# A float32 hybrid decoder trunk on one core: four small moves in order, banks and tables

## The chip, the core and the metric

The kernel runs on one core of a Trainium2 chip. The metric is device time in microseconds (us) of one execution, and the smaller is the better. The engines are named as in the profile: PE (TensorE, matmuls; PEld its weight loads), DVE (VectorE), ACT (ScalarE), POOL (GpSimd), SP (SyncE, which issues the DMAs of the weights).

## The reference

Two layers over 272 tokens (16 learned meta tokens and 256 others) of 1024 numbers, all in float32. Each layer norms its input, multiplies it by `w_in`, and splits the product into query latents (384), key-value latents (256), a rotary key (32), and the two halves of a recurrence (`xr` and `gt`, 512 each):

```python
for l in range(DEPTH):
    u = rmsnorm(h, norm_mix_g[l])
    cq, ckv, kr, xr, gt = jnp.split(u @ w_in[l], SPLITS, axis=-1)
    att = mla_mixer(cq, ckv, kr, cos, sin, ...)   # latents normed, 8 heads, causal blocks (0,16) (16,144) (144,272)
    rnn = rglru_mixer(xr, gt, ...)                # convolution, gates sigmoid(xb @ w_a), scan, times gelu(gt)
    h = h + concat(rmsnorm(att), rmsnorm(rnn)) @ w_out[l]
    u = rmsnorm(h, norm_ffn_g[l])
    h = h + (swiglu(u) if l % 2 == 0 else moe_swiglu(u))   # layer 0 dense, layer 1: top 2 of 8 experts
return h[:, N_META:]
```

The softmax of a head and query block is exp(s - max s) over its keys, divided by the sum. The cosine and sine of the rotary angles are computed once, from `positions`.

## The kernel before

**Matmuls of split floats.** Every large float32 weight is loaded by SP into one of four slots `raw`. ACT copies a piece of it, rounded, into `whi` (`split`, L984), DVE computes the rest `wlo` = `raw` - `whi` (`lo`, L1436), and PE makes three passes: high by high, high by low, low by high (L668 to L670 for the mixers and the dense part, L2551 and L2576 for the experts' first and second product). A piece can be split once the piece four before it in the ring has been used by PE; a slot of `raw` is free once its last `wlo` is done.

**Order.** Each engine has its own program, and the order of its instructions is the order of the code; nothing is scheduled by a tool. Engines wait on semaphores. The 8 PSUM banks are given out by `plan_blocks`: a block without a bank takes the next of banks 0 to 3 in turn, others are given one by hand (`GT_BANK`, `P_BANK`, `OUT_BANK`). PE waits in `fill` until the bank's last reader has signalled `emptied[bank]`.

**The part of a mixer where the latents are normed** (both layers). The blocks of `w_in` are computed in the order q, kv, kr, xr 0 to 3, gt 0. The first norm's root is a Sqrt on ACT (L1011). Behind block xr 1, PE sums the squares of the latents (`latss`). On ACT, each turn of the loop at L1071 splits the pieces that are due (`mix(l, *later(k))`). In the turn of (xr, 1), behind those splits, stand `tables()` (layer 0 alone: Sin of two angles, L1036 and L1038, and an Exp, L1040, that signals `splus_e`) and an empty `mark(ACT.Tanh)` of one element (L958), there for its table. In the turn of (xr, 2), ahead of the splits, stands `root_rows` (L1018), the Sqrt of the latents' sums. DVE takes the reciprocal of that root (`rows`, L1453) behind its own low piece of (xr, 1). PE, behind block xr 3, waits for it, spreads it over the partitions (`cqbc` and `kvbc`, L2047), computes gt 0, and goes on to the queries (L2156), for which DVE has multiplied the latents (L1513). Then come the recurrence's two sets of gates (L2175), four blocks each in the turning banks, which ACT empties with Tanh (L1113). Behind them ACT takes Exp of the decays (L1123), which waits for `vec_done`: 26 small operations on POOL (L843 to L857) that begin when `splus_e` is signalled.

**Attention.** `ATTENTION` lists the order per layer. `score(t)` (L2263) makes one block per head and query tile t, in the turning banks; DVE (`maxima`, L1598) adds the mask, scales and takes the maximum of a head in one custom instruction, ACT takes Exp with its sum per head (L1177). Tile 0 is the 16 meta tokens, and is computed in layer 0 alone. Between them DVE empties the `gt` blocks (`gelu_gate`, L1488) and computes the gate's gelu (L1681 to L1687). `values(t)` turns the probabilities of each head through PE (L2307, blocks `p` in banks 6, 7, 2 in turn), DVE and ACT by turns copy them out (`turned`, L1616 and L1187), and PE multiplies them by the values (L2322). DVE's program is written out by hand there: `gelu_gate(3)`, `gelu_times(1)`, then `turned(1, 0)`.

**Experts.** Each of the 8 experts runs 24 pieces: 16 of gate and up (L2551), then 8 of down (L2576) in `down(16)` to `down(23)`. The activated hidden state is turned through PE in two parts (L2563). ACT copies the second part's high half (`heh`, L1354) behind piece 19, and DVE subtracts it for the low half (`hel`, L1956) behind its own piece 19. Eleven chunks of 128 hidden units stand in the pieces of down; the last expert takes the pieces in another order (`in_turn`), so that its output's first half is done early, and there PE needs the second part of the turned state ahead of `down(18)`:

```python
down(17)
if gathers is not None:
    gather_low(gathers)
if not is_last(e):
    down(18, 19)
pe.wait_ge(xr_free[1], n0[1] + 3)     # hel is there
pe.wait_ge(xr_free[0], n0[0] + 4)
if is_last(e):
    down(18, 19)
down(20, 21, 22, 23)
```

## Time and profile before

| | |
|---|---|
| time, median of 3 runs | 895.87 us (894.41 to 896.41) |
| the profiled execution, its own time | 898.03 us |
| its span in the profile | 896.2 us |
| PE busy | 866.8 us (97%) |
| DVE busy | 683.6 us (76%) |
| ACT busy | 576.0 us (64%) |
| POOL busy | 70.8 us (8%) |
| granted TensorE clock, mean | 0.985 of full speed |
| moved by DMA | 208.70 MB, mean 233 GB/s |

The span goes from the first to the last recorded instruction or transfer; the execution's own time is 1.8 us longer. Matmuls are pipelined in the profile, so that PE's busy time is not a measure of its speed. The mixer of layer 0 lies at 0 to 150 us, the dense part up to 358 us, the mixer of layer 1 up to 486 us, and the experts take the rest.

### The profile page before, as it was taken

Reading aid. Unit: us, or ns where it says so; the run is one execution under the profiler, and the core shown is the slowest. Engines: PE = TensorE matmul, PEld = TensorE weight load, DVE = VectorE, ACT = ScalarE, POOL = GpSimd, SP = SyncE. Lnnn points to the kernel's source line nnn. Section 1 sums busy time; section 2 is a strip of 40 time slices with the busy share of each in tenths; the row PEclk is TensorE's granted clock in tenths of the full one; section 3 lists DMA queues with packets and bytes.
Section 4 is the critical chain, followed back from the end, with each engine's and each line's share of the span. In section 5 each row is a group of like instructions: output and inputs, shape, how many; then the busy total and the mean of one; then the engine's idle time right before and its main releaser. Section 6 shows DMA issues by size and latency. Waiting matters only on the chain.

```text
span 896.2 us, 15435 instructions
## 1 busy us (share of the span) xinstructions
PE 866.8 (97%) x5827; PEld 794.5 (89%) x5827; DVE 683.6 (76%) x914; ACT 576.0 (64%) x782; POOL 70.8 (8%) x93
## 2 busy tenths in 40 slices
PE   8989899999999999999899999999999999999995
PEld 7855789999999999965799989999998989999994
DVE  5667867766666555677877889789897998789883
ACT  6666746555454443666746777787778777777762
POOL 3530010000000000000042000000000000000001
PEclk9999899999999999999999999999999999999998
DMA  9505025555578553405055799899998999899981
GB/s 314 189 2 185 17 95 165 173 179 187 167 199 240 144 170 112 142 19 170 13 206 182 261 362 371 324 348 404 345 405 302 372 391 361 314 353 402 353 346 26
DMA packets 119436, 208.70 MB, mean 233 GB/s; under 512 B 5968, under 2 KB 71760, under 8 KB 119376
## 3 DMA queue, kind: packets, MB, share of 16 engines
q1 hardware_dynamic: 117232, 201.79, 63.7%
q0 software_dynamic: 1568, 5.24, 2.9%
q10 hardware_dynamic: 576, 0.87, 0.4%
q8 instruction: 38, 0.62, 0.3%
q14 instruction: 22, 0.18, 0.1%
HBM read 202.65 MB, written 5.24 MB: 232 GB/s over the span
## 4 chain that ended last, share of the span: by engine, by line
PE 85%; DVE 6%; ACT 4%; DMA 3%; issue 2%; POOL 0%; ACTq 0%; DVEq 0%; POOLq 0%; SPq 0%
PE ps L2551 27%; PE ps L2576 12%; PE ps L668 11%; PE ps L670 11%; PE ps L669 10%; PE ps L2156 2%; PE ps L2516 2%; DVE wlo L1436 2%; PE ps L2263 2%; PE ps L2322 1%; DMA raw<-in_w_in_dram 1%; PE ps L2047 1%; PE ps L2563 1%; DMA raw<-in_moe_w_down_dram 1%; DVE rr L1453 1%
## 5 line engine op out<-in xcount | busy, mean ns | idle before, releaser
L1436 DVE TENSOR_TENSOR wlo<-raw,whi 128x1536 fp32r<-128x1536 f32 (+4 forms) x298 | 437.9, 1495 | 90.5 <-ACT whi L984 88.2
L984 ACT ACTIVATE whi<-raw 128x1536 fp32r<-128x1536 f32 (+4 forms) x298 | 374.7, 1275 | 128.6 <-PE ps L670 58.1
L668 PE MATMUL ps<-uhi,whi 128*128 128x272 f32 (+1 forms) x576 | 170.3, 296 | 0.6 <-DVE wlo L1436 0.6
L670 PE MATMUL ps<-uhi,wlo 128*128 128x272 f32 (+1 forms) x576 | 166.8, 290 | 0.0
L669 PE MATMUL ps<-ulo,whi 128*128 128x272 f32 (+1 forms) x576 | 166.5, 289 | 0.0
L2551 PE MATMUL ps<-whi,xeh 128*128 128x320 f32 (+1 forms) x512 | 125.0, 325 | 0.0
L2551 PE MATMUL ps<-whi,xel 128*128 128x320 f32 (+1 forms) x512 | 123.5, 322 | 0.0
L2551 PE MATMUL ps<-wlo,xeh 128*128 128x320 f32 (+1 forms) x512 | 123.5, 322 | 0.0
L668 PEld LDWEIGHTS ps<-uhi,whi 128*128 128x128 f32 (+1 forms) x576 | 109.0, 189 | 4.2 <-issue 2.2
L669 PEld LDWEIGHTS ps<-ulo,whi 128*128 128x128 f32 (+1 forms) x576 | 109.2, 190 | 0.6
L670 PEld LDWEIGHTS ps<-uhi,wlo 128*128 128x128 f32 (+1 forms) x576 | 108.9, 189 | 0.0
L2551 PEld LDWEIGHTS ps<-whi,xeh 128*128 128x128 f32 x512 | 88.5, 188 | 0.7
L2551 PEld LDWEIGHTS ps<-wlo,xeh 128*128 128x128 f32 x512 | 89.0, 188 | 0.0
L2551 PEld LDWEIGHTS ps<-whi,xel 128*128 128x128 f32 x512 | 89.0, 188 | 0.0
L2576 PE MATMUL ps<-whi,heh 128*128 128x512 f32 x176 | 70.5, 401 | 2.4 <-DVE hel L1956 2.4
L2576 PE MATMUL ps<-wlo,heh 128*128 128x512 f32 x176 | 70.2, 399 | 0.0
L2576 PE MATMUL ps<-whi,hel 128*128 128x512 f32 x176 | 70.1, 399 | 0.0
L668 PE MATMUL ps<-ahi,whi 128*128 128x272 f32 x176 | 50.8, 289 | 0.0
L669 PE MATMUL ps<-alo,whi 128*128 128x272 f32 x176 | 50.7, 288 | 0.0
L670 PE MATMUL ps<-ahi,wlo 128*128 128x272 f32 x176 | 50.6, 287 | 0.0
L2576 PEld LDWEIGHTS ps<-whi,heh 128*128 128x128 f32 x176 | 33.4, 190 | 10.1 <-DVE hel L1956 2.9
L2576 PEld LDWEIGHTS ps<-whi,hel 128*128 128x128 f32 x176 | 33.4, 190 | 8.1
(314 smaller groups left out, 1200.3 us busy)
## 6 DMA issues: line engine op xcount, KB each, us to landing
raw<-in_moe_w_down_dram SPq DMA_DIRECT2D x24, 1536.0 KB, 9.2
raw<-in_moe_w_gate_dram SPq DMA_DIRECT2D x16, 1536.0 KB, 7.5
raw<-in_moe_w_up_dram SPq DMA_DIRECT2D x16, 1536.0 KB, 8.5
raw<-in_moe_w_gate_dram SPq DMA_DIRECT2D x16, 1280.0 KB, 10.1
raw<-in_moe_w_up_dram SPq DMA_DIRECT2D x16, 1280.0 KB, 9.4
raw<-in_ffn_w_gate_dram SPq DMA_DIRECT2D x11, 1024.0 KB, 5.2
raw<-in_ffn_w_up_dram SPq DMA_DIRECT2D x11, 1024.0 KB, 5.2
raw<-in_ffn_w_down_dram SPq DMA_DIRECT2D x8, 1408.0 KB, 6.9
```

The costliest lines, as they stand in the source:

```text
L668: pe.matmul(dst, wh, xh, start=start, stop=False, skip_group_check=True)
L669: pe.matmul(dst, wh, xl, start=False, stop=False, skip_group_check=True)
L670: return pe.matmul(dst, wl, xh, start=False, stop=stop, skip_group_check=True)
L984: act.activation(placed(whi, s, src), src, ACT.Copy).then_inc(hi_done, 1)
L1436: dve.tensor_tensor(placed(wlo, s, src), src, placed(whi, s, src).bitcast(F32), ALU.subtract).then_inc(lo_done, 1)
L1453: dve.reciprocal(rr[0:n, :], rr[0:n, :]).then_inc(rows_done, 1)
L2047: return pe.matmul(ps[0:width, bk, 0:T], ident[:, row:row + 1].to_broadcast([P, width]), rr[:, :], start=True, stop=True)
L2156: q = pe.matmul(bank(b, slice(width * i, width * (i + 1))), wq[:, k, c:c + width], cq[:, k, :], start=(k == 0), stop=(k == QC - 1), skip_g ...
L2263: pe.matmul(ps[0:n, b.bank, 0:lead + n], qT[0:QKH, h, lead:lead + n], kT[0:QKH, h, 0:lead + n], start=True, stop=True).then_inc(filled, 1)
L2516: m = pe.matmul(ps[:, b, c * 2 * P:(c + 1) * 2 * P], part[:, t * D + at:t * D + at + P], onehot[:, t, :, :], start=(t == 0), stop=(t == 1))
L2551: q = pe.matmul(ps[:, 2 * kind + n, 0:width], xs[:, kk, half, :], w[:, sl, at:at + width], start=(kk == 0 and xs is xeh and w is whi), sto ...
L2576: q = pe.matmul(ps[:, 4 + n, :], xs[:, kk, :], w[:, sl, at:at + 512], start=(kk == 0 and xs is heh and w is whi), stop=(kk == FEC - 1 and ...
```

## The change

Four edits:

1. On ACT, `tables()` and `mark(ACT.Tanh)` stand in the turn of (xr, 2), behind its split; so `root_rows` comes ahead of them, in both layers.
2. `GT_BANK` has a row per layer; in layer 1 the block gt 3 goes to bank 5, not 7.
3. The scores of the meta tokens (layer 0) are one block in bank 6: eight matmuls of 16 columns side by side. DVE masks, scales, takes the maxima and subtracts them in four operations over 16 x 8 x 16; ACT takes one Exp over them all, without a sum; DVE sums in `averages(0)`. The mask is added before the scale as before.
4. In the last expert, DVE computes the turned state's low half (`turned(6, TURN_B, 2)`) between pieces 18 and 19.

```diff
--- before.py
+++ after.py
@@ -208,7 +208,7 @@
 AHEAD = 2
 WARM = 5
 P_BANK = (6, 7, 2)
-GT_BANK = (6, 5, 4, 7)
+GT_BANK = ((6, 5, 4, 7), (6, 5, 4, 5))
 N_FF = 2 * (FF // GC) + KD
 MIX0 = [0, PER_MIX + N_FF]
 SPLIT0 = [0, MIX_SPLIT + 2 * N_FF]
@@ -258,10 +258,10 @@
             add("kbc", h)
         for what, t in ATTENTION[l]:
             if what == "scores":
-                for h in range(NH):
-                    add("s", t, h)
+                for h in range(NH if t else 1):
+                    add("s", t, h, bank=None if t else 6)
             elif what == "gt":
-                add("gt", t, bank=GT_BANK[t])
+                add("gt", t, bank=GT_BANK[l][t])
             elif what == "meta":
                 add("p", t, META, bank=6)
             elif what == "values":
@@ -1079,7 +1079,7 @@
                         act.activation(u32[:, QC:QC + KVC, :], ckv[:, :, :], ACT.Square).then_inc(squares, 1)
                         act.activation(kr[NOPE:QKH, 2, :], kr[NOPE:QKH, 0, :], ACT.Square).then_inc(krsq_done, 1)
                     mix(l, *later(k))
-                    if (name, c) == ("xr", 1):
+                    if (name, c) == ("xr", 2):
                         if not l:
                             tables()
                         mark(ACT.Tanh)
@@ -1199,6 +1199,10 @@
 
                 def exponentials(t, after=None):
                     act.wait_ge(sc_done, len(tiles(0)) * l + tiles(l).index(t) + 1)
+                    if not t:
+                        s = scores[0][0:NMETA, :, 0:NMETA]
+                        act.activation(s, s, ACT.Exp).then_inc(exp_done, NH)
+                        return
                     for h in range(NH):
                         exponential(t, h)
                         if after is not None:
@@ -1587,9 +1591,29 @@
 
                 dve.wait_ge(qscale_done, l + 1)
 
+                def meta_maxima():
+
+                    n = NMETA
+                    m0 = C_MASK + T - P
+                    b = B[l, "s", 0, 0]
+                    s = scores[0][0:n, :, 0:n]
+                    mask = con[0:n, m0:m0 + n].rearrange("p (h k) -> p h k", h=1).to_broadcast([n, NH, n])
+
+                    def of_head(row):
+                        return row.rearrange("p (h k) -> p h k", k=1).to_broadcast([n, NH, n])
+
+                    dve.wait_ge(filled, b.ready())
+                    dve.tensor_tensor(s, ps[0:n, b.bank, 0:NH * n].rearrange("p (h k) -> p h k", h=NH), mask, ALU.add)                       .then_inc(emptied[b.bank], 1)
+                    dve.wait_ge(emptied[b.bank], b.before + 1)
+                    link(dve.tensor_tensor(s, s, of_head(rt[0:n, 0, :]), ALU.mult))
+                    link(dve.tensor_reduce(small[0:n, 0, 0, :], s, AX.X, ALU.max))
+                    dve.tensor_tensor(s, s, of_head(small[0:n, 0, 0, :]), ALU.subtract).then_inc(sc_done, 1)
+
                 def maxima(t):
 
                     lead, n = TILES[t]
+                    if not t:
+                        return meta_maxima()
                     keys = lead + n
                     m0 = C_MASK + T - P - lead
                     for h in range(NH):
@@ -1620,6 +1644,8 @@
                     n = TILES[t][1]
                     o = osb_of(t)
                     dve.wait_ge(exp_done, NH * (len(tiles(0)) * l + tiles(l).index(t) + 1))
+                    if not t:
+                        link(dve.tensor_reduce(small[0:n, 0, 2, :], scores[0][0:n, :, 0:n], AX.X, ALU.add))
                     link(dve.reciprocal(small[0:n, t, 3, :], small[0:n, t, 2, :]))
                     b = B[l, "o", t]
                     dve.wait_ge(filled, b.ready())
@@ -1988,8 +2014,13 @@
                     turned(0, TURN_A, 1)
                     w(e, p, 16, 17)
                     times_up(1, HALF_B // 2)
-                    w(e, p, 18, 19)
-                    turned(6, TURN_B, 2)
+                    if is_last(e):
+                        w(e, p, 18)
+                        turned(6, TURN_B, 2)
+                        w(e, p, 19)
+                    else:
+                        w(e, p, 18, 19)
+                        turned(6, TURN_B, 2)
                     w(e, p, 20, 21, 22, 23)
                     if more:
                         w(e + 1, p, 0, 1, 2)
@@ -2252,8 +2283,22 @@
 
                 pe.wait_ge(qrot_done, l + 1)
 
+                def meta_scores():
+
+                    n = NMETA
+                    b = B[l, "s", 0, 0]
+                    fill(pe, b)
+                    for h in range(NH):
+                        kb = B[l, "kbc", h]
+                        pe.wait_ge(emptied[kb.bank], kb.before + 1)
+                        q = pe.matmul(ps[0:n, b.bank, n * h:n * (h + 1)], qT[0:QKH, h, 0:n], kT[0:QKH, h, 0:n],
+                                      start=True, stop=True)
+                    q.then_inc(filled, 1)
+
                 def score(t):
                     lead, n = TILES[t]
+                    if not t:
+                        return meta_scores()
                     for h in range(NH):
                         b = B[l, "s", t, h]
                         fill(pe, b)
```

ACT's program in layer 0, from the squares of the latents to the split ahead of the queries; before:

```order
L1080 ACTIVATE kr<-kr 32x272
L984 ACTIVATE whi<-raw 128x1024 x2
L1036 ACT_TABLE_LOAD
L1036 ACTIVATE sinT<-rope 128x272
L1038 ACTIVATE cosT<-rope 128x272
L1040 ACT_TABLE_LOAD
L1040 ACTIVATE spt<-spt 128x8
L958 ACTIVATE scr<-one 128x1
L1018 ACT_TABLE_LOAD
L1018 ACTIVATE rr<-ps,eps 64x272
L958 ACTIVATE scr<-one 128x1
L984 ACTIVATE whi<-raw 128x1024 x2
```

and with the change:

```order
L1080 ACTIVATE kr<-kr 32x272
L984 ACTIVATE whi<-raw 128x1024 x2
L1018 ACTIVATE rr<-ps,eps 64x272
L958 ACTIVATE scr<-one 128x1
L984 ACTIVATE whi<-raw 128x1024
L1036 ACT_TABLE_LOAD
L1036 ACTIVATE sinT<-rope 128x272
L1038 ACTIVATE cosT<-rope 128x272
L1040 ACT_TABLE_LOAD
L1040 ACTIVATE spt<-spt 128x8
L958 ACTIVATE scr<-one 128x1
L984 ACTIVATE whi<-raw 128x1024
```

The latents' root (L1018) with its mark stands three table loads and four activations sooner and has no load of its own; of the two splits behind it (L984) one has moved ahead of the tables. Further on, the load that stood at the gates' first Tanh (L1113) is gone as well, in both layers; in layer 1 the one at `mark(ACT.Tanh)` now stands behind the root.

DVE's program for the last expert, from the pieces 16 and 17 to its end; before:

```order
L1436 TENSOR_TENSOR wlo<-raw,whi 128x1536 x2
L1970 SCALAR_TENSOR_TENSOR hact<-act,slotg,ps 128x640
L1436 TENSOR_TENSOR wlo<-raw,whi 128x1536
L1436 TENSOR_TENSOR wlo<-raw,whi 128x1024
L1956 TENSOR_TENSOR hel<-ps,heh 128x512
L1956 TENSOR_TENSOR hel<-ps,heh 128x128
L1436 TENSOR_TENSOR wlo<-raw,whi 128x1536 x3
L1436 TENSOR_TENSOR wlo<-raw,whi 128x1024
```

and with the change:

```order
L1440 TENSOR_TENSOR wlo<-raw,whi 128x1536 x2
L1996 SCALAR_TENSOR_TENSOR hact<-act,slotg,ps 128x640
L1440 TENSOR_TENSOR wlo<-raw,whi 128x1536
L1982 TENSOR_TENSOR hel<-ps,heh 128x512
L1982 TENSOR_TENSOR hel<-ps,heh 128x128
L1440 TENSOR_TENSOR wlo<-raw,whi 128x1024
L1440 TENSOR_TENSOR wlo<-raw,whi 128x1536 x3
L1440 TENSOR_TENSOR wlo<-raw,whi 128x1024
```

The two subtractions for `hel` (L1956, in the change L1982) stand ahead of the 128x1024 piece, which is piece 19.

DVE's program at the meta tokens' scores, behind gt 1, its beginning before (the pair of L1598 comes eight times, once per head):

```order
L1488 TENSOR_TENSOR gt<-ps,rsb 128x272
L1529 ISA
L1598 ISA u,small<-ps,con,rt 16x16
L1598 ISA small 16x1
L1598 ISA u,small<-ps,con,rt 16x16
L1598 ISA small 16x1
L1598 ISA u,small<-ps,con,rt 16x16
```

and with the change, down to the next tile's first pair:

```order
L1492 TENSOR_TENSOR gt<-ps,rsb 128x272
L1533 ISA
L1606 TENSOR_TENSOR u<-ps,con 16x8x16
L1608 TENSOR_TENSOR u<-u,rt 16x8x16
L1609 TENSOR_REDUCE small<-u 16x8
L1610 TENSOR_TENSOR u<-u,small 16x8x16
L1622 ISA u,small<-ps,con,rt 128x144
L1622 ISA small 128x1
```

Sixteen custom instructions and the sign's turn (L1606) have become four operations.

## Rows read from the trace of the kernel before

**Rows 1.** The page: the chain that ended last, shares of the span by engine
```profile
PE 85%; DVE 6%; ACT 4%; DMA 3%; issue 2%; POOL 0%; ACTq 0%; DVEq 0%; POOLq 0%; SPq 0%
```

**Rows 2.** Waits of PE over the whole run: us in total, times, longest
```profile
PE ps L2047 <- DVE rr L1453: 3.1, 2, 2.9
...
PE ps L2576 <- DVE hel L1956: 2.4, 1, 2.4
PE ps L2307 <- DVE gt L1488: 2.4, 1, 2.4
PE ps L2175 <- ACT ta L1113: 2.1, 2, 1.1
```

**Rows 3.** Timeline of ACT, layer 0: start, us, engine line op, [idle before <- releaser]
```profile
38.79 1.28 ACT L1036 ACT_TABLE_LOAD   x1
...
43.75 0.48 ACT L1018 ACTIVATE rr<-ps,eps 64x272 f32<-64x272 f32 x1
...
59.16 1.28 ACT L1113 ACT_TABLE_LOAD   x1
...
63.61 2.12 ACT L1123 ACTIVATE xr<-ta,nsp 128x272 f32<-128x272 f32 x4
```

**Rows 4.** Timeline of DVE, layer 0, at the latents' root
```profile
44.50 1.84 DVE L1453 RECIPROCAL rr<-rr 64x272 f32<-64x272 f32 x1 [1.79 <-ACT scr L958]
```

**Rows 5.** Timeline of PE, layer 0: block xr 2's first matmul, and the spread
```profile
37.26 0.39 PE L668 MATMUL ps<-uhi,whi 128*128 128x272 f32 x1
...
46.40 2.18 PE L2047 MATMUL ps<-rr,con 128*128 128x272 f32 x4 [2.87 <-DVE rr L1453]
```

**Rows 6.** Stretches: length, busy of PE, PEld, DVE, ACT, POOL, clock, DMA share, GB/s
```profile
60.00:63.00 3.00, 2.01 (x8) 1.43 (x8) 0.00 (x0) 2.99 (x8) 0.00 (x0) 1.00 0.00 0
382.60:386.87 4.27, 4.18 (x32) 3.87 (x36) 4.20 (x10) 1.02 (x1) 0.08 (x1) 1.00 0.01 4
46.40:52.10 5.70, 5.70 (x32) 5.09 (x36) 5.60 (x11) 0.00 (x0) 4.66 (x13) 0.72 0.00 0
```

**Rows 7.** Timeline of DVE, layer 1, at the latents' root
```profile
380.80 1.84 DVE L1453 RECIPROCAL rr<-rr 64x272 f32<-64x272 f32 x1
```

**Rows 8.** Timeline of POOL: the chain behind `splus_e`, its first, an inner one, its last
```profile
42.45 0.37 POOL L843 TENSOR_SCALAR spt<-spt 128x8 f32<-128x8 f32 x1 [8.70 <-ACT spt L1040]
...
46.71 1.28 POOL L851 TENSOR_SCALAR spt<-spt 128x8 f32<-128x8 f32 x1
...
54.57 0.46 POOL L857 TENSOR_SCALAR nsp<-spt 128x8 f32<-128x8 f32 x1
```

**Rows 9.** Timeline of DVE: first scores of metas and of tiles 1 and 2; turned block
```profile
88.65 0.22 DVE L1598 CUSTOM_DVE_ANT_0 u<-ps,con,rt 16x16 f32<-16x16 f32 x1 [0.16 <-DVE gt L1488]
...
90.11 0.37 DVE L1598 CUSTOM_DVE_ANT_0 u<-ps,con,rt 128x144 f32<-128x144 f32 x1
...
97.30 0.50 DVE L1598 CUSTOM_DVE_ANT_0 ksq<-ps,con,rt 128x272 f32<-128x272 f32 x1 [0.82 <-PE ps L2263]
...
114.22 0.42 DVE L1616 COPY pT<-ps 128x256 f32<-128x256 f32 x1 [1.89 <-PE ps L2307]
```

**Rows 10.** The same of layer 1: tile 1's first head, tile 2's fifth
```profile
423.44 0.37 DVE L1598 CUSTOM_DVE_ANT_0 u<-ps,con,rt 128x144 f32<-128x144 f32 x1 [0.16 <-PE ps L2263]
...
429.12 0.50 DVE L1598 CUSTOM_DVE_ANT_0 ksq<-ps,con,rt 128x272 f32<-128x272 f32 x1 [0.77 <-PE ps L2263]
```

**Rows 11.** Timeline of PE, layer 1: the first product with the values
```profile
438.71 0.64 PE L2322 MATMUL ps<-vt,pT 128*128 128x64 f32 x2 [0.81 <-DVE pT L1616]
```

**Rows 12.** Timeline of DVE, last expert: piece 19 and `hel`
```profile
873.23 1.23 DVE L1436 TENSOR_TENSOR wlo<-raw,whi 128x1024 fp32r<-128x1024 f32 x1 [0.29 <-ACT whi L984]
874.38 0.88 DVE L1956 TENSOR_TENSOR hel<-ps,heh 128x512 fp32r<-128x512 f32 x2
```

**Rows 13.** The chain that ended last, as pieces: start, us, what; nine matmuls each
```profile
820.61 2.09 PE ps L2576 x9
...
875.36 3.89 PE ps L2576 x9
```

## The prediction

> **What bounds the kernel.** I read the chain that ended last first: 85% of the span is PE's, and DVE and ACT stand in it only where PE waits [rows 1]. So a step is worth what it takes from a wait of PE, or from the tail behind PE's last matmul. Then the waits of PE: the four that matter here are the latents' root (L2047, 2.9 us of the 3.1 in one place), the second set of gates (L2175, 2.1 us in two), the last expert's `hel` (L2576, 2.4 us) and gt 3's bank (L2307, 2.4 us) [rows 2]. Then the timelines at these places, and the granted clock of the stretches behind them, because PE runs there at half clock: 46.40 to 52.10 us was granted 0.72 of full speed on the mean, its twin in layer 1 1.00 [rows 6]. Half is 1.2 GHz, full 2.4 GHz.
>
> **Edit 1, the root, layer 0.** ACT begins its first table load at 38.79 us and reaches the root at 43.75, behind three loads of 1.28 us and four small activations [rows 3]. Now the root comes first and without a load, so it starts at about 38.8, and its 0.48 us and the mark are over by 39.5. DVE's reciprocal had waited 1.79 us for it [rows 4]; DVE itself is late next, and begins at 44.50 - 1.79 = 42.71. PE's spread stood at 46.40 [rows 5] and moves by the same: **1.8 us**. The queries behind it need DVE's products with the latents, which follow the reciprocal in DVE's program and move too.
>
> What is moved behind the root: the tables now wait for the split of block xr 2's turn, which waits for PE to finish that block. It begins at 37.26 us [rows 5] and 24 matmuls take 3.0 us (an estimate from one every 0.125 us in that timeline), so the split runs from about 40.3 to 41.3, and the tables to about 45.0. The next split, of gt 3, comes at about 45.2, where before it came at about 45.4: nothing. POOL's chain began at 42.45 behind the Exp and ended at 54.57 + 0.46 = 55.0 [rows 8]; it shifts to 45.0 and ends at about 57.6. ACT needs it for the decays, at 63.61 before [rows 3], and at about 59.3 if everything below comes true. Cover 1.7 us: nothing. No DMA is moved by any edit, and SP's queue keeps its order; weights due after the mixers are asked for when PE and DVE free their slots, so they shift with the rest.
>
> **Edit 1, layer 1.** DVE's reciprocal at 380.80 shows no idle ahead of it [rows 7]: the root was in time, and its earlier place gives nothing.
>
> **Edit 1, the gates, both layers.** The load at 59.16 us [rows 3] stands in front of the first Tanh on the gates, while PE waits for the bank that this Tanh empties: 1.1 us of PE's 2.1 in the longer case, so about 1.05 each [rows 2]. The table is now there already. Without the load a Tanh (about 0.4 us) is shorter than PE's gate block (2.10 / 4 = 0.52 us by the timeline), and the wait goes: **2.1 us** for two layers, of 2.56 us of loads. The bounds are 0 (another wait takes over) and 2.56. I take 2.1, since ACT is busy without a gap in both layers behind it and PE's next wait, the second root's, hangs on ACT.
>
> The Trainium skill's page ScalarE: Activation LUTs, section What ACT_TABLE_LOAD costs, gives 1.28 us for the load and another 1.38 us of drain at every switch. By it the two loads would give 2.8 us more. This trace disagrees: three loads and four activations fit in the 4.96 us from 38.79 to 43.75, where three times 2.66 us would not.
>
> **Edit 2, the bank of gt 3.** PE waited 2.4 us for it, but then 0.81 us more, to 438.71, for the first turned head, which DVE copies behind gt 3 and two gelu operations [rows 2, 11]. Only the turning of heads 1 and 2 gets ahead; the first product still starts where DVE lets it. **0 us**; at best 0.4 (heads copied by ACT sooner), and PE's two gaps become one.
>
> **Edit 3, the metas' scores.** Sixteen custom instructions and a sign took DVE from 88.65 to 90.11, 1.46 us [rows 9]. The four new ones have 128 elements per partition; the 16-wide one took 0.22, the 144-wide one 0.37 [rows 9], and each waits for the one before. At 0.29 each that is 1.16: **0.3 us**; the bounds are 0.6 (four at 0.22) and a loss of 0.3 (four at 0.45). PE's eight matmuls no longer wait for four banks, so tile 1's first scores are in time. ACT's seven Exps fewer lie in time when it waits for DVE. The new sum in `averages(0)`, some 0.2 us, stands ahead of DVE's wait of 1.89 us for PE at 114.22 [rows 9]: nothing; without that cover it would cost its 0.2.
>
> **Edit 4, the last expert.** DVE began piece 19 at 873.23 and `hel` at 874.38 [rows 12]. `hel` now comes first, but ACT's copy `heh` stands behind ACT's split of piece 19, whose end 873.23 marks; with some 0.4 us for that copy (as DVE's 0.88 / 2 on the same bank), `hel` starts at about 873.6: **0.8 us** on PE's start at 875.36 [rows 13]. Bounds 0.5 and 1.15. Piece 19 is late by 0.9 us, to about 875.6; PE needs it nine matmuls behind `down(18)`, at 876.7 or later.
>
> Sum without the clock: 1.8 + 2.1 + 0 + 0.3 + 0.8 = 5.0 us.
>
> **The clock.** Behind an idle of 2.87 us the stretch from 46.40 took 5.70 us, its twin of layer 1 4.27 [rows 5, 6]: 1.4 us. Behind the 2.4 us in the last expert nine matmuls took 3.89 us, against 2.09 in the expert before [rows 2, 13]: 1.8 us. From tile 1's first head to tile 2's fifth layer 0 took 97.30 - 90.11 = 7.19 us, layer 1 429.12 - 423.44 = 5.68 [rows 9, 10]: 1.5 us. Now the first idle shrinks to 2.87 - 1.79 = 1.1 us, that of the last expert to 1.6. A gap of 1.1 us at the gates left the clock at 1.00 in 60 to 63 us [rows 2, 6]. 1.1 is that case, and 1.6 is nearer to it than to 2.4, so I count both as kept at full clock: 3.2 us. At the scores the gap ahead of tile 1 goes, but the small matmuls of the metas stay; I count nothing.
>
> **Sum** 5.0 + 3.2 = 8.2 us, against the profiled execution's 898.03 us: 889.8. The median of the runs shown is 2.16 us below that execution. Taken from the median, as the runs will be: 895.87 - 8.2 = **887.7 us**. Whether the runs of the median had all these half-clock stretches isn't shown; the range has to hold that.
>
> **Rivals.**
> - *The clock stays low behind the shorter gaps*, as in each of the longer ones. Then 5.0 us are left: 890.9. For it: one profile shows only one gap near 1.1 us. Chance 0.25.
> - *The scores of layer 0 get full clock too*: 8.2 + 1.5 = 9.7, 886.2. For it: layer 1, without metas, kept it [rows 10]. Chance 0.18.
> - *A switch of tables costs more than its load*: if ACT stood still at each as long again as the load takes, the two loads in PE's way would give 2 x 1.28 = 2.6 us more, 885.1. The 4.96 us above for three loads and four activations speak against it. The Trainium skill's page named above, ScalarE: Activation LUTs, says as much, with its own figure. Chance 0.02.
> - *The gains are swallowed* in the mixers by another chain (DVE's convolutions, the two weights' landings) and the tail stays: 895, within 0.2%. A table load left ahead of the root would be its other form, but the order shows none. Chance 0.03.
> - *Slower: POOL's chain.* It starts 2.6 us later. If it ends behind ACT's need at 59.3, ACT, and all behind it, wait. Some of its operations are held: 1.28 us at 46.71 against 0.37 and 0.46 for its like [rows 8]. At 0.9 us each, two more held ones reach the need at 59.3; eleven, to 67.5, would cancel the whole gain, and thirteen give 897.7. In the Trainium skill's GPSIMD Engine Reference, section Key points, POOL shares its SBUF interfaces with DVE and contends with DVE instructions that read two inputs from SBUF; by that rule DVE's low pieces hold it, and they move along with it. But only a few of the 26 operations can meet one. Chance 0.02.
>
> **How the numbers follow.** Forecast 0.47, the rivals 0.50; the other 0.03 I give to smaller gains, near 892.5. From 885.0 to 892.0 the range holds the forecast, both clock rivals, and the bounds of edits 2 to 4 (0.4 and -0.3, 0.6 and -0.3, 1.15 and 0.5); a new half-clock stretch elsewhere, 1.5 us more on 890.9, is left outside. A measurement of this kernel can tell about 0.2%, 1.8 us, from no change. Faster by more: 0.95; within: 0.03; slower: 0.02.
>
> **What would show it.** ACT's L1018 root at about 38.8 us with no load ahead; DVE's reciprocal at about 42.7 with no wait; PE's spread at about 44.5 and clock 1.00 behind it; no wait of PE at the gates (L2206 in the change) in either layer; PE's first product with the values of layer 1 as long behind gt 3 as before; four operations on DVE in place of 1.46 us; PE's wait for `hel` at 1.6 us and nine matmuls in 2.1 us behind it. I am wrong if the reciprocal still waits for ACT, if ACT waits for POOL at the decays, or if half-clock stretches as long as before follow.

## The result, and the profile after

The changed kernel took 887.51 us (median of 10 runs, 886.57 to 891.36), the kernel before beside it 896.18 (median of 10, 894.27 to 902.41). The ratio is 0.990, its 95% interval 0.9873 to 0.9927: faster by 8.7 us, and by 6.5 to 11.4. The forecast was 8.2 us less and 887.7.

The profiled execution took 886.6 us, its span 884.7. That is 11.5 us under the span of before, more than the medians differ by. 1.8 of it is the start: DVE's low piece ahead of the reciprocal begins at 39.65 us, in the trace of before at 41.49, and nothing ahead of it was changed. What follows is therefore read as distances from that point.

The page's part 1, busy time, and the head of part 4, the chain's shares by engine:

```profile
PE 861.0 (97%) x5827; PEld 789.6 (89%) x5827; DVE 682.6 (77%) x902; ACT 568.0 (64%) x763; POOL 72.8 (8%) x93
...
PE 86%; DVE 6%; DMA 3%; ACT 2%; issue 1%; POOL 0%; ACTq 0%; DVEq 0%; POOLq 0%; SPq 0%
```

ACT's share of the chain went from 4% [rows 1] to 2%: layer 0's root with the three table loads ahead of it, and the load at the gates of each layer, are no longer in it. Two loads of 1.28 us (L958, at 68.53 and 399.87 us) still are. The waits of PE over the whole run (line <- releaser: us in total, times, longest):

```profile
PE ps L2367 <- DVE pT L1640: 3.8, 3, 3.4
...
PE ps L2621 <- DVE hel L1982: 1.2, 1, 1.2
PE ps L2078 <- DVE rr L1457: 1.0, 2, 0.8
```

Against [rows 2], the root's wait fell from 3.1 to 1.0 us, that for `hel` from 2.4 to 1.2, the one at the gates (L2206 now) is gone, and the one for gt 3's bank (2.4) has become part of a wait for the first turned head (3.4).

Timeline of ACT, layer 0 (start, us, engine line operation, [idle before <- releaser]):

```profile
36.84 0.47 ACT L1018 ACTIVATE rr<-ps,eps 64x272 f32<-64x272 f32 x1
...
39.87 1.07 ACT L984 ACTIVATE whi<-raw 128x1024 fp32r<-128x1024 f32 x1 [2.33 <-DMA raw<-in_w_in_dram]
40.95 1.28 ACT L1036 ACT_TABLE_LOAD   x1
42.25 0.43 ACT L1036 ACTIVATE sinT<-rope 128x272 f32<-128x272 f32 x1
...
53.81 1.62 ACT L1113 ACTIVATE ta<-ps,hba 128x272 f32<-128x272 f32 x4
...
57.31 2.13 ACT L1123 ACTIVATE xr<-ta,nsp 128x272 f32<-128x272 f32 x4 [0.17 <-POOL nsp L857]
```

The root has no load ahead and the Tanh (53.81) none either, as the prediction had it. Two things it did not have: the split ahead of the tables waited for its DMA and not for PE, so the tables came 1.4 us later than worked out; and ACT did wait for POOL at the decays, 0.17 us. DVE and PE at the same place:

```profile
40.79 1.84 DVE L1457 RECIPROCAL rr<-rr 64x272 f32<-64x272 f32 x1
```

```profile
42.68 1.18 PE L2078 MATMUL ps<-rr,con 128*128 128x272 f32 x4 [0.82 <-DVE rr L1457]
...
52.59 3.94 PE L2206 MATMUL ps<-xc,gdiag 128*128 128x272 f32 x16
```

The reciprocal's idle of 1.79 [rows 4] is gone. PE's idle is 0.82 in place of 2.87, and its four matmuls take 1.18 us in place of 2.18 [rows 5]: full clock. At the gates sixteen matmuls run in one piece.

Timeline of DVE, layer 0, the metas' scores, tile 1's first head, tile 2's fifth:

```profile
82.04 0.28 DVE L1606 TENSOR_TENSOR u<-ps,con 16x128 f32<-16x128 f32 x1
82.35 0.28 DVE L1608 TENSOR_TENSOR u<-u,rt 16x128 f32<-16x128 f32 x1
82.67 0.28 DVE L1609 TENSOR_REDUCE small<-u 16x8 f32<-16x128 f32 x1
82.97 0.28 DVE L1610 TENSOR_TENSOR u<-u,small 16x128 f32<-16x128 f32 x1
83.19 0.35 DVE L1622 CUSTOM_DVE_ANT_0 u<-ps,con,rt 128x144 f32<-128x144 f32 x1
...
88.86 0.50 DVE L1622 CUSTOM_DVE_ANT_0 ksq<-ps,con,rt 128x272 f32<-128x272 f32 x1 [0.77 <-PE ps L2308]
```

The four operations take 83.19 - 82.04 = 1.15 us (estimated 1.16, before 1.46). From tile 1's first head to tile 2's fifth it is 5.67 us, where [rows 9] had 7.19: the half clock at the scores is absent from this trace. Five stretches, three at full clock and two at half (start and end, length, busy time of PE with its instructions, granted clock, DMA share, GB/s):

```profile
42.70:46.80 4.10, 4.10 (x28) 1.00 0.00 2
97.30:104.10 6.80, 6.59 (x27) 0.50 0.00 1
424.77:428.40 3.63, 0.49 (x5) 0.99 0.21 72
428.40:435.20 6.80, 6.50 (x27) 0.50 0.00 1
865.31:867.41 2.10, 2.10 (x9) 1.00 0.00 0
```

Behind the root and in the last expert the clock is whole. At the values of layer 0 the stretch is as long as before. At the values of layer 1 it is 6.8 us, where the trace of before had 3.4: behind one gap of 3.4 us in place of two.

### The profile page after: what moved, and what is told of

It reads as the page before. It is cut to its first block, busy times and chain, and to the rows that moved or that the text cites. A ratio compares the mean times of both kernels' runs of the same rounds, so it can differ in the third digit from the quotient of the medians.

```text
span 884.7 us, 15398 instructions
## 1 busy us (share of the span) xinstructions
PE 861.0 (97%) x5827; PEld 789.6 (89%) x5827; DVE 682.6 (77%) x902; ACT 568.0 (64%) x763; POOL 72.8 (8%) x93
## 4 chain that ended last, share of the span: by engine, by line
PE 86%; DVE 6%; DMA 3%; ACT 2%; issue 1%; POOL 0%; ACTq 0%; DVEq 0%; POOLq 0%; SPq 0%
PE ps L2596 27%; PE ps L2621 12%; PE ps L668 11%; PE ps L670 11%; PE ps L669 11%; PE ps L2187 2%; DVE wlo L1440 2%; PE ps L2561 2%; PE ps L2367 1%; PE ps L2308 1%; DMA raw<-in_w_in_dram 1%; PE ps L2608 1%; PE ps L2078 1%; PE ps L2206 1%; DMA raw<-in_moe_w_down_dram 1%
## 5 line engine op out<-in xcount | busy, mean ns | idle before, releaser
L984 ACT ACTIVATE whi<-raw 128x1536 fp32r<-128x1536 f32 (+4 forms) x298 | 374.5, 1275 | 131.1 <-PE ps L670 58.6
```

What stands on the lines that cost most here:

```text
L984: act.activation(placed(whi, s, src), src, ACT.Copy).then_inc(hi_done, 1)
```

## Experiments

All times are medians; each ratio is to the kernel before, run beside it on the same chip. Since that kernel's medians lay between 895.5 and 898.2 us, the ratios are what is compared. The changed kernel's is 0.9900. The intervals are 3 to 5 us wide, so a part of under 2 us is read from traces, and the times only say that nothing larger is hidden.

**Each edit undone in turn.** First the tables ahead of the root again:

```
-                    if (name, c) == ("xr", 2):
+                    if (name, c) == ("xr", 1):
                         if not l:
                             tables()
                         mark(ACT.Tanh)
```

> The change without its first edit: the two Sines, their tables and the Tanh table stand ahead of the latents' root again. The prediction's terms: 1.8 us (reciprocal behind the root) and 2.1 us (table load at the gates) come back, and the 1.4 us that the clock lost behind the root's gap, 5.3 in all: 892.8 us. Rival, the clock's part is no property of this gap: the half-clock stretch appears in one place or another whatever the gap does, 3.9 us alone, 891.4. In the trace: the Sine load ahead of L1018, the reciprocal with an idle of about 1.8, PE's spread with about 2.9, the Tanh load inside the gates.

894.82 us, ratio 0.9981 (0.9957 to 1.0005): 7.3 us of the 8.7 are lost, where 5.3 were expected and 3.9 by the rival. The first edit is most of the change. Its profiled execution took 1697 us, each matmul 1.6 times as long, and its trace says nothing of the edit (the twelve other executions took 892.9 to 901.0). So it was run again for a trace:

> The change without its first edit once more, for a trace of it (its profiled execution took 1697 us, each matmul 1.6 times as long, and tells nothing of the edit). Theory one (the prediction): reciprocal's idle 1.8 us, PE's spread 2.9 us, PE's wait at the gates 2.1 us in two places, and half clock behind the root. What the run of times showed beyond that (7.2 us against the 5.3 of the terms) is then a further stretch of half clock, in the gates or the scores. Rival: a wait of PE that the prediction does not have, of about 1.9 us in all.

The one execution took 898.79 us. Timeline of PE, and a wait of PE, in its trace:

```profile
44.49 2.18 PE L2078 MATMUL ps<-rr,con 128*128 128x272 f32 x4 [2.70 <-DVE rr L1457]
```

```profile
PE ps L2206 <- ACT ta L1113: 2.1, 2, 1.1
```

The reciprocal's idle is 1.80 us, and PE's waits are the old ones and no others, so the rival with a further wait falls. There is more half clock instead: 6.8 us of it at the scores, in a kernel whose metas' scores are already in one bank.

Then the bank:

```
-GT_BANK = ((6, 5, 4, 7), (6, 5, 4, 5))
+GT_BANK = ((6, 5, 4, 7), (6, 5, 4, 7))
```

> The change without its second edit: layer two's last gate block is in bank 7 again. The prediction's term is 0 (at most 0.4 us slower): 887.5 to 887.9 us. Rival, from the trace of the changed kernel: there one wait of PE of 3.3 us stands where two of 2.4 and 0.8 stood, and behind it 6.83 us of half clock where 3.41 were; if the one longer gap makes the longer stretch, the bank's return gives 1.3 us back (the values of tile 1 and 2 advanced by 10.0 us ahead of it and by 8.7 behind it): 886.2, with 3.41 us of half clock in this place.

887.9 us, ratio 0.9892 (0.9869 to 0.9915): nothing. Timeline of PE, layer 1:

```profile
427.75 0.44 PE L2352 MATMUL ps<-con,u 128*128 128x128 f32 x2 [2.39 <-DVE gt L1492]
...
429.00 0.41 PE L2367 MATMUL ps<-vt,pT 128*128 128x64 f32 x2 [0.81 <-DVE pT L1640]
```

The two gaps are back, and half clock still stands behind them for 6.8 us, from 429.6. So a stretch of 6.8 us does not need the one longer gap: my rival, drawn from a single pair of traces, falls.

Then the metas' scores, head by head in eight blocks of the turning banks (the planner's blocks and the four branches on `not t` taken out):

> The change without its third edit: the metas' scores in eight banks, with their operations head by head. The prediction's term is 0.3 us: 887.8 us. Rival, from the trace of the changed kernel: the half-clock stretch that stood at the scores of layer 0 (90.6 us) is gone there, and the time between DVE's first head of tile 1 and the fifth of tile 2 fell by 1.5 us; if the eight small groups made it, they bring back 1.5 us beside the 0.3: 889.3, with a stretch of 3.41 us of half clock at the scores of layer 0.

887.85 us, ratio 0.9905 (0.9875 to 0.9935): no difference that can be measured. In its trace DVE needs 11.87 us from the second reciprocal to tile 1's first head, against 11.52 in the changed kernel: 0.35 us. It has half clock at the scores for 6.83 us, but at the values of layer 1 for only 3.4. The half clock at the scores is what the rival asked for (it expected 3.41 us of it); the time does not show its 1.5 us, and its interval of 5 us could hide them.

Then DVE's order in the last expert:

```
-                    if is_last(e):
-                        w(e, p, 18)
-                        turned(6, TURN_B, 2)
-                        w(e, p, 19)
-                    else:
-                        w(e, p, 18, 19)
-                        turned(6, TURN_B, 2)
+                    w(e, p, 18, 19)
+                    turned(6, TURN_B, 2)
```

> The change without its fourth edit: in the last expert VectorE takes the split of piece 19 ahead of the turned half again. The prediction's terms: 0.8 us of PE's wait and 1.8 us of the clock in the nine matmuls behind it come back: 890.1 us. Rival, the clock did not follow from this gap: 0.8 us alone, 888.3 us, and the nine matmuls take 2.1 us in the trace.

891.08 us, ratio 0.9928 (0.9904 to 0.9953): 2.5 us lost, and 3.2 against the two kernels above on the same chip. Timeline of DVE and of PE in its trace:

```profile
864.77 1.23 DVE L1440 TENSOR_TENSOR wlo<-raw,whi 128x1024 fp32r<-128x1024 f32 x1 [0.26 <-ACT whi L984]
865.91 0.88 DVE L1982 TENSOR_TENSOR hel<-ps,heh 128x512 fp32r<-128x512 f32 x2
```

```profile
866.89 0.77 PE L2616 MATMUL ps<-whi,heh 128*128 128x512 f32 x1 [2.50 <-DVE hel L1982]
```

From ACT's split of piece 18 to PE's start it is 5.66 us here, 5.69 before, and 4.98 to 5.06 in seven traces with the edit on DVE alone: the edit's own part is 0.6 us. The clock comes on top: the next nine matmuls take 3.5 us here and 2.2 in the changed kernel. The two are 1.9 us together; the rest of the 2.5 or 3.2 is within the intervals.

**The first edit in halves.** Only the Tanh table moves behind the root:

```
-                    if (name, c) == ("xr", 2):
-                        if not l:
-                            tables()
+                    if not l and (name, c) == ("xr", 1):
+                        tables()
+                    if (name, c) == ("xr", 2):
                         mark(ACT.Tanh)
```

> Only half of the first edit: the two Sines, the Exp and their tables stay ahead of the latents' root, and only the load of the Tanh table is behind it. The prediction splits the first edit into the root (1.8 us, and 1.4 us of clock behind it) and the gates (2.1 us). By it the gates' part is kept and the root's lost: 887.6 + 3.2 = 890.8 us, some 6 under the kernel before. Rival, the root's shift is worth more than its terms (the change without its first edit came out at 894.8, 7.2 above the 887.6 of the change, where 5.3 were expected): if the surplus of 1.9 lies with the root, 892.7; if it lies with the gates, 890.8. No wait of PE at the gates (L2206) in either case.

891.85 us, ratio 0.9932 (0.9907 to 0.9957): 2.9 us over the changed kernel, where 3.2 were expected. By the times the gates hold 4.4 of the 7.3 us, within intervals of that size. The price of a load there shows without any noise in the distance between DVE's two reciprocals (latents' root to scores' root):

```
                                   layer 0    layer 1
before, and a second trace     33.74, 33.77   32.22, 32.22
first edit undone                     33.68          32.21
only the Tanh table behind            30.89          30.87
changed kernel                        30.88          30.88
```

That is 1.34 us in layer 1, where a share of 1.05 was predicted. In layer 0 PE's gates, from their first matmul to the next product, take 5.21 us with the load and 3.86 without: the same 1.35. This leaves 33.74 - 30.88 - 1.34 = 1.5 us more in layer 0, the half clock behind the root. Root and clock together are 3.3 us, the gates 2.7. But PE's spread in this kernel:

```profile
44.61 1.18 PE L2078 MATMUL ps<-rr,con 128*128 128x272 f32 x4 [2.91 <-DVE rr L1457]
```

The same gap of 2.9 us as before, and full clock behind it. So that gap alone does not bring the half clock.

**POOL's chain.** Eight operations more, which change no value, and then the chain begun sooner:

```
             link(pool.tensor_tensor(w, w, z, ALU.mult))
+            for _ in range(8):
+                link(pool.tensor_scalar(w, w, 1.0, None, ALU.mult))
```

> Eight operations more in POOL's chain (a factor of one, in place). The price of the slower rival: the chain ends at 57.3 us in the changed kernel and ScalarE waits 0.17 us for it at the decays. Eight more at 0.23 us each make 1.8 us, at 0.45 us each (as those beside VectorE's convolutions) 3.6. If TensorE has no slack behind the decays, all of it shows: 889.4 to 891.2 us. If ScalarE's work behind the decays is needed later than it is done, less than 0.9 shows: 887.6 to 888.5. The wait of L1123 for POOL grows to 2.0 to 3.8 us in both.

889.13 us, ratio 0.9919 (0.9893 to 0.9945), 1.7 us over the changed kernel. ACT, and the waits of PE that are new, in its trace:

```profile
60.16 2.13 ACT L1125 ACTIVATE xr<-ta,nsp 128x272 f32<-128x272 f32 x4 [3.33 <-POOL nsp L859]
```

```profile
64.29 1.98 PE L2249 MATMUL ps<-raw,osb 128*128 128x512 f32 x4 [1.50 <-DVE kr L1551]
...
71.22 0.67 PE L2267 MATMUL ps<-ksq,con 128*32 128x272 f32 x8 [1.33 <-ACT scr L960]
```

The distance between the reciprocals grew by 33.84 - 30.88 = 2.96 us for a wait of 3.33. PE has next to no slack behind the decays: the slower rival's price is right, nine parts in ten. The medians show 1.7 of the 2.96 us. Whether something came back is not shown, as the interval is 5 us wide; in the traced execution, alone among the thirteen, there is no half clock at the values of layer 0.

```
             def tables():
+                act.wait_ge(splus, 1)
+                act.activation(spt[:, 1, :], spt[:, 0, :], ACT.Exp, scale=-1.0).then_inc(splus_e, 1)
...
-                act.wait_ge(splus, 1)
-                act.activation(spt[:, 1, :], spt[:, 0, :], ACT.Exp, scale=-1.0).then_inc(splus_e, 1)
```

> The Exp that starts POOL's chain goes ahead of the two Sines, with its table: the chain starts about 2.1 us sooner. ScalarE's wait of 0.17 us at the decays goes. The prediction's view (the cover is just enough): 887.4 to 887.6 us, no difference that can be measured. Rival: the Sines come 0.2 to 2.1 us later for VectorE's rotations, which wait for them: slower by up to 1 us, 888.6.

888.85 us, ratio 0.9897 (0.9879 to 0.9915). The wait is gone and the distance between the reciprocals is 30.94 us: the 0.17 us had cost nothing, and the cover is just enough.

**The last expert, ScalarE too.**

```
-                    w(e, p, 19)
-                    turned(6, TURN_B)
+                    if is_last(e):
+                        turned(6, TURN_B)
+                        w(e, p, 19)
+                    else:
+                        w(e, p, 19)
+                        turned(6, TURN_B)
```

> In the last expert ScalarE too takes the turned half ahead of piece 19 (the change moves it on VectorE alone, whose split waits 0.79 us for it). The copy starts at the end of piece 18's split, 0.97 us sooner, and so does TensorE, whose wait for hel was 1.23 us: 886.6 us, with a wait of 0.26 left. Rival: piece 19 is then late for TensorE, or bounds the tail in its place: 887.6, and a wait for whi or wlo of 0.5 us or more nine matmuls behind.

887.18 us, ratio 0.9885 (0.9863 to 0.9907), 1.3 us under the changed kernel's ratio. ACT and DVE in its trace:

```profile
863.10 0.74 ACT L1358 ACTIVATE heh<-ps 128x512 fp32r<-128x512 f32 x2
```

```profile
864.90 0.88 DVE L1986 TENSOR_TENSOR hel<-ps,heh 128x512 fp32r<-128x512 f32 x2
```

From ACT's split of piece 18 to PE's start it is now 4.18 us, 0.87 less (the same in the two kernels below that share the edit), with full clock behind. The term of 1.0 was nearly right. The wait of PE is still 1.7 us, not 0.26, because piece 18 itself landed late: ACT waited 3.2 us for it here, 2.3 in the changed kernel's trace.

**A second trace of the kernel before.**

> The kernel before once more, for a second trace of it. Theory one, the stretches of half clock belong to the gaps that the prediction put them behind: again 3.4 us each behind the root (46 us), at the scores of layer 0 (90 us) and behind the last expert's hel. Theory two, they belong to an execution as well as to a gap: one or more of them is gone or elsewhere, though the gaps are the same to 0.1 us. The stretch at the very start (full clock from 12.1 us, against 5.6 to 8.5 in six traces of the changed kernels) tells whether the start too differs by execution: then it is below 9 us here.

896.63 us, span 894.7. DVE's reciprocal begins at 42.60 us (44.50 in the first trace), so the start alone differs by 1.9 us between executions. PE's waits are the same to 0.1 us. The stretches (columns as above):

```profile
45.37:48.78 3.41, 3.41 (x16) 0.50 0.00 0
88.00:92.00 4.00, 4.00 (x26) 1.00 0.14 16
```

Half clock behind the root again, but none at the scores, with the metas in eight blocks as in the first trace. At the values of layer 1 it has 6.8 us of it, where the first had 3.4. The second theory holds: where the clock falls differs between two executions of one program with the same gaps.

**Layer two's heads sooner.** The changed kernel with the last expert's edit on both engines, and in layer two this order on DVE; on ACT its first turned head goes ahead of its split, its second ahead of the Tanh of block 2:

```
+                    turned(1, 0)
                     mix(l, N_IN)
                     gelu_gate(3)
+                    turned(1, 2)
                     gelu_times(1)
-                    turned(1, 0)
                     gelu_inner(2)
-                    turned(1, 2)
+                    turned(1, 4)
                     gelu_inner(3)
-                    turned(1, 4)
-                    gelu_times(2)
                     turned(1, 6)
-                    gelu_times(3)
+                    gelu_times(2)
                     turned(1, META)
+                    gelu_times(3)
```

> The change, with ScalarE's turned half of the last expert sooner, and in layer two the copies of tile 1's turned heads ahead of the gate work: VectorE's first ahead of the split and the last gate block, its second ahead of two gelu operations, ScalarE's first ahead of its split. PE's wait of 3.4 us for the first turned head falls to about 0.7, a second one for head 1 or 2 of 1.5 to 2 takes part of it back. If VectorE's order was the limit (the prediction's reason why the second edit is worth 0): 1.0 to 1.5 us less than with the tail alone (0.9885 of before), 884.5 to 885.2 us, and 1.5 more where the shorter gap keeps the clock, 883.0. Rival: the gelu work that is now later holds the RNN's output and the values of tile 2: 886 to 887.

886.78 us, ratio 0.9903 (0.9885 to 0.9922): a miss, no gain over the tail alone (0.9885). Timeline of PE:

```profile
425.40 0.41 PE L2393 MATMUL ps<-vt,pT 128*128 128x64 f32 x2 [0.99 <-DVE pT L1653]
...
427.12 0.69 PE L2393 MATMUL ps<-vt,pT 128*128 128x64 f32 x2 [0.84 <-DVE pT L1653]
...
430.14 0.69 PE L2393 MATMUL ps<-vt,pT 128*128 128x64 f32 x2 [0.41 <-ACT pT L1187]
```

The gap of 3.4 us became four of 0.3 to 1.0, 2.5 together, and half clock came all the same, from 427.0 for 6.8 us. From tile 1's first head to tile 2's first turned block DVE needs 21.48 us, against 21.66 to 21.92 in seven other traces with bank 5 and as long a stretch. The same with bank 7:

> The same as the kernel before it, with the second edit undone: layer two's last gate block in bank 7 again. Now the block stands in the way of head 1's turning, which has to wait for VectorE's read of it, and no head copy is ahead to hide that. If the second edit was worth 0 only because VectorE's order came first, this is slower than the kernel with bank 5 by 0.5 to 1.5 us. Rival, the bank never matters: the same within 0.5 us.

887.83 us, ratio 0.9913 (0.9895 to 0.9931), 1.0 us over its twin. Timeline of PE:

```profile
428.20 0.44 PE L2378 MATMUL ps<-con,u 128*128 128x128 f32 x2 [2.60 <-DVE gt L1505]
```

The same distance on DVE is 22.45 us, 0.97 more than with bank 5. Here the bank matters, because the heads' copies no longer stand behind gt 3. The times, 1.0 us apart, agree, but that is less than their intervals.

## Why the prediction was right, point by point

**Edit 1, the root: right.** 1.8 us, and DVE was late next. Layer 1 gave nothing at the root, as said.

**Edit 1, the gates: right in mechanism, too small in size.** The step "1.1 us of PE's 2.1 in the longer case, so about 1.05 each" took PE's visible wait for the price. It is 1.34 us in layer 1 and 1.35 in layer 0, 2.7 in all in place of 2.1, and above the bound of 2.56 that I had drawn from the loads alone. The load is 1.28 of it; what the other 0.06 is, no run shows. The Trainium skill's page ScalarE: Activation LUTs, section What ACT_TABLE_LOAD costs, puts a switch at about 2.66 us with its drain. The runs disagree with this: a switch in PE's way cost 1.34 us, and the Sine begins 1.30 us after its load's start.

**Edit 1, POOL's chain: the term of nothing came true, its reason only just.** The step "the split ... waits for PE to finish that block" failed: it waited for its DMA. One of the prediction's signs of being wrong, that ACT waits for POOL at the decays, did come, with 0.17 us that cost nothing. In the terms of before, the chain began at 46.4 us in place of 45.0, ran 12.7 us (12.6 before), and used up the cover of 1.7 us and 0.17 more. The timeline of POOL shows what the operations cost, by what DVE does beside them:

```profile
44.60 0.25 POOL L843 TENSOR_SCALAR spt<-spt 128x8 f32<-128x8 f32 x1 [9.97 <-ACT spt L1040]
...
48.33 0.46 POOL L847 TENSOR_TENSOR spt<-spt 128x8 f32<-128x8 f32 x1
...
49.95 0.29 POOL L851 TENSOR_SCALAR spt<-spt 128x8 f32<-128x8 f32 x1
...
55.15 0.23 POOL L851 TENSOR_SCALAR spt<-spt 128x8 f32<-128x8 f32 x1
...
57.05 0.23 POOL L857 TENSOR_SCALAR nsp<-spt 128x8 f32<-128x8 f32 x1
```

```profile
48.23 1.58 DVE L1501 SCALAR_TENSOR_TENSOR xc<-xr,vec,xc 128x272 f32<-128x272 f32 x3
49.72 0.42 DVE L1499 TENSOR_SCALAR xc<-xr,vec 128x272 f32<-128x272 f32 x1
```

0.41 to 0.48 us beside DVE's three operations with two tensors from SBUF, 0.29 beside its operation with one, 0.20 to 0.27 from 54.3 us on, with DVE mostly idle. By the GPSIMD Engine Reference of the Trainium skill, section Key points, POOL contends with such DVE instructions; the trace agrees. I gave the slower rival 0.02. Its price per microsecond was right (2.96 for 3.33), and another 2 us on the chain would have taken a fifth of the gain.

**Edit 2: right.** 0 us, for the reason given: DVE's order was ahead of the bank. The last pair of kernels shows the reason itself, with 1.0 us for the bank once DVE's order is out of the way.

**Edit 3: right.** 0.35 us by the traces, 0.3 predicted; by the times nothing.

**Edit 4: right in kind, its term too large.** 0.6 us and not 0.8 (bounds 0.5 and 1.15). The step "some 0.4 us for that copy" was short: from the start of ACT's copy (863.72 us) to `hel` (864.32) it is 0.60. Piece 19 was to be late by 0.9 us, but the end given for it, 875.6, is 1.1 us behind the 873.23 + 1.23 of before; no wait of PE came from it. "PE's wait for `hel` at 1.6" is not one number: in seven traces with the edit on DVE alone it is 1.2, 1.7, 1.8, 1.9, 1.9, 2.5 and 2.8 us, by how late piece 18 lands.

**The clock: right behind the root, half right in the last expert.** These are the gaps of PE at the two places in all thirteen traces, and what stood behind them:

```
gap of PE, us                                    half clock behind it
root, 2.70, 2.87, 2.88                           3 of 3
root, 2.91                                       none
root, 0.62 to 1.21                               0 of 9
hel, 2.35, 2.45, 2.46, 2.50, 2.84                5 of 5
hel, 1.85, 1.86                                  1 of 2
hel, 1.00 to 1.77                                0 of 6
```

The step "I count both as kept at full clock" holds for the root, where it is worth 1.5 us (1.4 predicted). In the last expert four of those seven traces kept it, so the 1.8 us, of which 1.5 are clock by the trace of before (nine matmuls at the place took 3.7 us against 2.2), are worth about 0.9 on the mean. By the second trace of before, where the nine took 3.2 us, it would be 0.6. That root gaps of 2.7 to 2.9 us go with half clock and those up to 1.2 without is shown as a tendency, with one exception.

**The rivals.** "The clock stays low behind the shorter gaps" fell. "The scores of layer 0 get full clock too" looks right in the trace of after, but one pair of traces cannot show it: a second trace of before has full clock there as well, and one of the change without its first edit has 6.8 us of half clock there. Counted over all thirteen, half clock stands at the scores in two of the three traces with the metas in eight blocks and in one of the ten with a single block. The kernel without the third edit takes the same time, within an interval of 5 us. So the third edit may bear on it; whether it does stays open, and the sum below has nothing for it.

**The sum.** 1.8 + 2.7 + 0.35 + 0.6 = 5.4 without the clock (5.0 predicted), 1.5 + 0.9 with it: 7.8 us, where the medians differ by 8.7 with an interval of 6.5 to 11.4. The predicted total of 8.2 lies between, helped by an overcount in the tail (2.6 against 1.5) that the undercount at the gates made good in part. The mechanisms of the four edits are shown; that the forecast of 887.7 us came within 0.2 us of the measured 887.51 is luck, with intervals of 5 us and clock terms that differ by 1 us or more from one execution to the next. The run without the first edit lost 7.3 us where its terms make 6.0. The two intervals cover that difference, and whether something is left in it stays open.

## What to carry to other kernels

Price a table load that stands in the bottleneck engine's way at its own duration, not at the wait that is visible in one place, and look for a spot where the engine waits for data anyway. When something is moved behind a step, ask of every instruction in between what it waits for, its transfers too, because the cover of a side chain is measured from there. Before a half-clock stretch is booked as a gain, take a second trace of the same kernel. Behind gaps of 2.3 us and more half clock came nearly every time here, but a short gap is no guarantee of full clock: in twelve of the thirteen traces half clock also begins at the choice of the experts in layer 1 (at 476.15 us in the changed kernel; 3.4 or 6.8 us long), where PE's longest gap in the 25 us before is 0.54 us and its work just before is transposes and products of 1 to 16 columns.

## What was not expected of the hardware

Two executions of one program part within the first 45 us by 1.9 us: full clock came at 12.1 us in the first trace of before, at 7.8 in the second, and at 5.6 to 8.5 us in the eleven of the other kernels.

Half clock moves between places without any change of the work: between the two traces of before, at layer 1's values from 3.4 us to 6.8, at layer 0's scores from 3.4 to none. Over all thirteen traces the scores have none, 3.4 or 6.8. The distance on DVE from tile 1's first head to tile 2's first turned block is 24.11 and 22.47 us in the two traces of before, and in layer 1 20.56 and 21.66. In this pair layer 1 lost 1.1 of the 1.6 us that layer 0 won. This is why a single pair of traces named an effect of the bank, which the runs refute, and one of the metas' scores, which they leave open.

The version with the last expert's turned half ahead of piece 19 on both engines has the lowest ratio of those run, 0.9885. Its gain over the change, 1.3 us, is within the intervals; what three traces show is that PE starts 0.87 us sooner behind ACT's split of piece 18.
